# Up block first in seven-product feed-forward cells, three open pairs, and longer DRAM rows for the cells' weights

## The chip, the cores and the metric

One Trainium2 chip, all 8 cores, one launch. Each core computes one prompt stream and two sample streams with the whole set of weights; nothing passes between cores. The metric is the device time in microseconds of the slowest core.

## What is computed

One encoder layer, for 8 prompt streams of 8192 frames (one per core) and 16 sample streams of 32 frames, D = 1024, FFN width 2816. Cut to what matters:

```python
z = x @ w_in                                   # u | v | B | C | x_in
v = layernorm per head(v);  a = u * (masked W_s mixes v over 128 frames + b_s)
b = gb * causal_conv3(gc * xin)
x = layernorm(ALPHA * x + concat(a, b) @ w_out)
p = softmax((x @ w_q) @ mem_k.T / 16);  x = layernorm(ALPHA * x + (p @ mem_v) @ w_mem_o)
f = (silu(x @ w_gate) * (x @ w_up)) @ w_down   # the change is here
x = layernorm(ALPHA * x + f)
```

## The kernel before, in words

A core works through 16 tiles of 512 frames. Part A of a tile (`run_A`) is the input projection with mixers, the output projection, attention scores, and the attention output, its weights in a ring of three 1 MB slots (`ra`). Part B (`run_B`) is the feed-forward block: 11 cells of 256 FFN columns (`gate_up` or `gate_up_7`), then `down` in six pieces. Their weights go through the ring `rb` of 16 units of 128 x 1024 elements, 256 KB each. Part A of tile t+1 runs interleaved with part B of tile t.

In tiles 0 and 1 a cell is plain (32 matmuls of 512 columns). From tile 2 on it is made of seven products instead of eight (a Winograd form of the 2 x 2 block product): `gate_up_7` issues seven groups `prod` of 8 matmuls of 256 columns. The four weight blocks of a cell are a11, a12, a22 (parts `gu` 0 to 2) and a21; four sums of them, s1 to s4 (parts `gs` 0 to 3), are made by VectorE in tile 2 (`weight_sums`, line 981), and four differences of the activations (T1, T3, T4, in `early`, and one in F2) by `row_sums` in each tile. The products accumulate in a pair of PSUM banks, ba and bb, with evacuations between them: ScalarE copies M1 from bb into `s5`, then ba into bb (bank<-bank), applies silu to ba for the gate half into `sg`; VectorE adds bb and s5 into ba and into s5, and two multiplications write hT (the last one's line is 1032). There are two buffers s5 and four sg, two per cell, so two cells' pairs can be open.

Weights are cast to 16 bits once, by GpSimd's DMAs from `w_pieces` (line 633), stored by SP into a DRAM scratch `wsc` of rows of 8 KB per partition and piece (line 609), and loaded from it later: whole pieces into `ra` (line 628), single units with rows of 2 KB into `rb` (`load_unit`, line 616). The sums are stored as pieces gs0 to gs10 in tile 2. A cell of a later tile loads seven single units in the order in which the products use them (`CELL`).

The other transfers: SP stores y of a tile in four parts (line 1062) and loads the next x, 2 MB, into the same buffer (line 688), after the last of these stores has landed. GpSimd loads the transposed x (line 673). From tile 3 on ScalarE issues DMA transposes of the layer-normed rows (line 774, F<-xb), eight a tile.

The order of the instructions on each of the five queues is written out by a planner (`Sched.order`), an event simulation with priorities (`S.prio`, lower first, plus `dprio`) and durations (`c_v`, `c_a`, `c_mm`). It models buffers by name (`buf`): an operation that writes a buffer depends on all its former writers and readers, DMAs among them. What it emits is static: each engine runs its list in order and waits on semaphores. Most instructions are recorded through `Resolving.call`, line 89, so rows of the profile are told apart by their tiles.

Of the kernel before, what the change touches and what calls it, by code (L numbers as in the profile page):

```python
# [8 lines left out]
BF16 = mybir.dt.bfloat16  # L9
FP16 = mybir.dt.float16  # L10
AF = mybir.ActivationFunctionType
ALU = mybir.AluOpType
# [117 lines left out]
class Sched:  # L130
# [73 lines left out]
    def order(self):  # L204
# [81 lines left out]
        while ev:  # L286
# [44 lines left out]
            if o.dma:  # L331
                occ = 1.0 if e == "gpsimd" else 0.08
                rings[e].append([o.nbytes, t + occ + 0.6, o])
                dma_step(t)
            else:
                occ = o.dur
                if e == "scalar" and o.table is not None:
                    if table is not None and o.table != table:
                        occ += 1.4
                    table = o.table  # L340
                o.fin = t + occ
# [89 lines left out]
KV_PIECES = ["m0", "m1", "n0", "n1"]  # L431
SUM_PIECES = ["gs%d" % j for j in range(NF // 2)]
STORE_AT = {"in_v": 2, "in_c0": 2, "in_c1": 2, "in_c2": 2, "in_c3": 2, "out0": 2, "out1": 2}
# [8 lines left out]
def build(NT, debug=False):  # L442
# [33 lines left out]
    widx = {n: i for i, n in enumerate(W_PIECES)}  # L476
    SP_PIECES = A_PIECES + B_PIECES + KV_PIECES + SUM_PIECES
    sidx = {n: i for i, n in enumerate(SP_PIECES)}
    wsc = nc.dram_tensor("wsc", [len(SP_PIECES), 128, 4096], BF16, kind="Internal").ap()

    with contextlib.ExitStack() as st:
        def T(name, shape, dt):
            return st.enter_context(nc.sbuf_tensor(name, shape, dt))
# [54 lines left out]
        TB = [early[:, i * 1024:(i + 1) * 1024].bitcast(FP16).rearrange("p (k n) -> p k n", k=4) for i in range(3)]  # L538
        s5 = [early_t[:, 1536 + i * 512:2048 + i * 512] for i in range(2)]
        guard_t = T("guard", [1, 1], F32)  # L540
        def bank(p):
# [44 lines left out]
        def units(n, step):  # L586

            u = -(-rctr["B"] // step) * step % NU
            while u + n > NU and step > 1 or any(("B", (u + i) % NU) in pinned for i in range(n)):
                u = (u + step) % NU  # L590
            rctr["B"] = u + n
            return [(u + i) % NU for i in range(n)]

        def unit(u):
            return rb[:, u * 1024:(u + 1) * 1024], buf("ringB%d" % u)
# [16 lines left out]

        def load_unit(name, n, u, dprio=-0.35):

            src, (dst, b) = wsc[sidx[name]], unit(u)
            op("sync", lambda e: e.dma_start(out=dst, in_=src[:, n * 1024:(n + 1) * 1024]), [buf("wsc_" + name)], [b],  # L616
               dma="rB%d" % u, nbytes=1 << 18, dprio=dprio)

        def piece(r, name, t, dprio=-0.35):
            i, dst, b = slot(r)  # L620
            nco = piece_cols(name)
            gu = name[:2] == "gu"
            if name in stored and r == "B":
                for n in range(nco // 1024):
                    load_unit(name, n, i + n, dprio)
            elif name in stored:
                src = wsc[sidx[name]]
                op("sync", lambda e: e.dma_start(out=dst[:, 0:nco], in_=src[:, 0:nco]), [buf("wsc_" + name)], [b],
                   dma="r%s%d" % (r, i), nbytes=256 * nco, dprio=dprio)
            else:  # L630
                src = wp[widx[name]]
                to = dst[:].bitcast(FP16) if gu else dst
                op("gpsimd", lambda e: e.dma_start(out=to[:, 0:nco], in_=src[:, 0:nco]), [], [b],
                   dma="f%s%d" % (r, i), nbytes=512 * nco, pkt=16, dprio=dprio)
                if t == 0:
                    buf("ld_" + name).writers = [S.ops[-1]]
                if name in sidx and t >= STORE_AT.get(name, 0):
                    store(name, dst, b, "w%s%d" % (r, i), nco)
            return (dst[:].bitcast(FP16) if gu else dst), b

        CELL = (("gs", 0), ("gu", 0), ("gu", 1), ("gs", 1), ("gs", 2), ("gs", 3), ("gu", 2))

        def cell_units(j):

            out = {}
            for (kind, n), u in zip(CELL, units(7, 1)):
                load_unit("%s%d" % (kind, j), n, u)
                v, b = unit(u)
                out[kind, n] = (v.bitcast(FP16), b)
            return out  # L650

        def cell_parts(rg, brg, sm, bsm):
            return {(kind, n): ((rg, sm)[kind == "gs"][:, n * 1024:(n + 1) * 1024], (brg, bsm)[kind == "gs"][n]) for kind, n in CELL}

# [136 lines left out]
        def in_proj_v(c, rg, brg, parts=None):  # L791
# [19 lines left out]
            for s in range(4):  # L811
                bk, bb = bank(c.pl)
                for k0, k1, bp in parts:
                    MM([(bk[:], c.F0[:, k, s * 128:(s + 1) * 128], rg[:, k * 512:(k + 1) * 512], k == 0, k == 7) for k in range(k0, k1)],
                       [buf(c.pre + "F0_%d" % s), brg, bp], [bb], 512)

                def out(i, h, bk=bk, bb=bb, s=s):
                    A(lambda e: e.activation(out=c.vh[:, s, h * 128:(h + 1) * 128], in_=bk[:, h * 128:(h + 1) * 128],
                                             func=AF.Identity, scale=rs[i][:, h:h + 1], bias=nm[i][:, h:h + 1]),
                      [bb, buf("rs%d" % i), buf("nm%d" % i)], [buf(c.pre + "vh%d" % s)], 128)  # L820
                sgu_v(bk, bb, 128, out)

        def in_proj_c(c, m, rg, brg):
# [39 lines left out]
            else:  # L863
                A(lambda e: e.activation(out=halo_p[:, m, :], in_=cx3[:, 0, L:L + 2], func=AF.Copy), [bcx], [buf("halo_p%d" % m)], 2)
            A(lambda e: e.activation(out=ac3, in_=cx3[:, :, 0:L], func=AF.Copy, scale=smallT[:, w0:w0 + 1]), [bcx, buf("small")], [bac], n)
            for k in (1, 2):
# [75 lines left out]
        def plain(g, f2, k):  # L942

            b_ = ((0, 1), (3, 2))[g][k // 4]
            return slice(b_ * 1024 + (k % 4) * 256 + f2 * 128, b_ * 1024 + (k % 4) * 256 + (f2 + 1) * 128)
# [27 lines left out]
        def weight_sums(j, rg, brg):  # L973
# [6 lines left out]
            for o_, x_, y_, f_ in ((s1, a21, a22, ALU.add), (s3, a11, a21, ALU.subtract), (s2, s1, a11, ALU.subtract), (s4, a12, s2, ALU.subtract)):  # L980
                V(lambda e, o_=o_, x_=x_, y_=y_, f_=f_: e.tensor_tensor(out=o_, in0=x_, in1=y_, op=f_), [brg] + ([b] if f_ is ALU.subtract else []), [b], 512)
            store("gs%d" % j, raw, b, "wB%d" % i)
            return dst, b
# [13 lines left out]
        def gate_up_7(c, j, w):  # L997
# [7 lines left out]
            def prod(bk, w, x, reads, writes, first):  # L1005
# [7 lines left out]
                op("tensor", fn, reads, writes, dur=c_mm(8, 256))  # L1013
            i5, ia, ib = rot("s5", 2), rot("sg", NSG), rot("sg", NSG)
            b5, bsa, bsb = buf("s5_%d" % i5), buf("sg%d" % ia), buf("sg%d" % ib)
            pair = lambda x: x.rearrange("p (f n) -> p f n", f=2)
            bh = [buf("hT%d" % f) for f in (2 * j, 2 * j + 1)]
            prod(bb, s1, t1, [bs1, buf("T1")], [bbb, bba], True)
            A(lambda e: e.activation(out=s5[i5], in_=bb[:], func=AF.Copy), [bbb], [b5], 512)
            prod(ba, a11, b11, [ba11] + F2b[:2], [bba], True)  # L1020
            A(lambda e: e.activation(out=bb[:], in_=ba[:], func=AF.Copy), [bba], [bbb], 512)
            prod(ba, a12, b21, [ba12] + F2b[:2], [bba], False)
            prod(bb, s2, t2, [bs2] + F2b[2:], [bbb], False)
            A(lambda e: e.activation(out=sg[ia][:], in_=ba[:], func=AF.Silu), [bba], [bsa], 512, table="silu")
            V(lambda e: e.tensor_tensor(out=ba[:], in0=bb[:], in1=s5[i5], op=ALU.add), [bbb, b5], [bba], 512)
            prod(bb, s3, t3, [bs3, buf("T3")], [bbb], False)
            prod(ba, s4, b22, [bs4] + F2b[2:], [bba], False)
            V(lambda e: e.tensor_tensor(out=s5[i5], in0=bb[:], in1=s5[i5], op=ALU.add), [bbb, b5], [b5], 512)
            A(lambda e: e.activation(out=sg[ib][:], in_=ba[:], func=AF.Silu), [bba], [bsb], 512, table="silu")
            prod(bb, a22, t4, [ba22, buf("T4")], [bbb], False)  # L1030
            V(lambda e: e.tensor_tensor(out=hT[:, 2 * j:2 * j + 2, H1], in0=pair(bb[:]), in1=pair(sg[ia][:]), op=ALU.mult), [bbb, bsa], bh, 512)
            V(lambda e: e.tensor_tensor(out=hT[:, 2 * j:2 * j + 2, H2], in0=pair(s5[i5]), in1=pair(sg[ib][:]), op=ALU.mult), [b5, bsb], bh, 512)

# [254 lines left out]
        def run_B(tiles, t):  # L1288
            n = NF // 2
            for j in range(n):  # L1290
# [14 lines left out]
                if t == T_SUMS:  # L1305
                    w = cell_parts(rg, brg, *weight_sums(j, rg, brg))
                for c in tiles:
# [54 lines left out]
def make_in_maps(inputs, NT):  # L1362
# [29 lines left out]
    for j in range(NF // 2):  # L1392
        sl = slice(j * 256, (j + 1) * 256)
        blocks = [kpn(w) for w in (wg[0:512, sl], wg[512:1024, sl], wu[512:1024, sl], wu[0:512, sl])]
        pieces[W_PIECES.index("gu%d" % j)] = np.concatenate(blocks, axis=1)
# [55 lines left out]
```

How the kernel before makes its waits and increments, by code:

```python
                def body(eng, ops=ops, e=e):  # L401
                    view = Resolving(eng)
                    waited = {}
                    dwaited = {}
                    for o in ops:
                        for pe_, d in o.best.items():
                            if waited.get(pe_, 0) < d.sig:
                                eng.wait_ge(sems[pe_], d.sig)
                                waited[pe_] = d.sig
                        for s, c in o.dmadeps.items():
                            if dwaited.get(s, 0) < c:
                                eng.wait_ge(dsems[s], c)
                                dwaited[s] = c
                        inst = o.fn(view if o.leases else eng)
                        if o.dma:
                            inst.then_inc(dsems[o.stream], 16)
                        elif o.signal:
                            inst.then_inc(sems[e], 1)
                    if e == final_wait_eng:
                        for s, c in total.items():
                            if dwaited.get(s, 0) < c:
                                eng.wait_ge(dsems[s], c)
```

## Time and profile before

| What | us |
|---|---|
| median of three runs | 3643.74 |
| lowest, highest run | 3566.81, 3689.93 |
| the profiled execution | 3604.81 |
| its span on the slowest core (3) | 3603.3 |
| spans of the eight cores | 3561.5 to 3603.3 |

The profile is of one execution, on its slowest core. Busy time of TensorE is modelled from pipelined matmuls. PEclk is the clock granted to TensorE as a share of 2.4 GHz. In a row of waits, the instruction named first waited for the one behind the arrow.

### The profile page before, as it was taken

What the parts mean: (1) busy time and instruction counts of PE and PEld (TensorE: products, weight loads), DVE (VectorE), ACT (ScalarE), POOL (GpSimd) and SP (SyncE); (2) the same over time, 40 slices, a digit from 0 to 9 for tenths busy, and PEclk for the clock granted to TensorE, in tenths of its full rate; (3) what the DMA queues carried; (4) which work ended last, traced back from release to release, by engine and by line L of the source; (5) the groups of instructions that cost most, each with busy time, mean ns of one, the idle gap of its engine ahead of it and who ended that gap; (6) DMA issues with size and microseconds to landing.
All of it is one profiled execution on the core that took longest, in us unless ns stands there. A gap on an engine that the chain in (4) does not pass through costs nothing.

```text
span 3603.3 us, 59509 instructions; the slowest of 8 cores (3561.5 to 3603.3 us)
## 1 busy us (share of the span) xinstructions
PE 3243.4 (90%) x19332; PEld 1878.9 (52%) x19332; DVE 1970.8 (55%) x3564; ACT 1071.3 (30%) x1781; POOL 381.3 (11%) x357
## 2 busy tenths in 40 slices
PE   7989999869989897998989899897988899899887
PEld 3544444544555645555555555555555464555564
DVE  5753435645646565554746655464564656456443
ACT  4452123142232422313232232322323242232320
POOL 2111101001001010100101110010110101010000
PEclk9999988978899999999989999998999999999987
DMA  9879887786777869687786877868787786968684
GB/s 180 165 170 198 188 221 195 214 160 182 224 207 205 221 184 256 183 233 199 187 232 196 234 211 224 206 184 223 196 225 216 208 222 187 247 185 224 178 230 122
DMA packets 367182, 731.43 MB, mean 203 GB/s; under 512 B 138464, under 2 KB 138592, under 8 KB 335520
## 3 DMA queue, kind: packets, MB, share of 16 engines
q1 hardware_dynamic: 243664, 623.12, 59.7%
q0 software_dynamic: 12240, 75.13, 12.3%
q10 hardware_dynamic: 110976, 29.37, 6.3%
q8 instruction: 163, 2.67, 0.3%
q14 instruction: 139, 1.14, 0.1%
HBM read 694.73 MB, written 76.43 MB: 214 GB/s over the span
## 4 chain that ended last, share of the span: by engine, by line
PE 68%; DMA 24%; issue 2%; DVE 1%; ACTq 1%; ACT 1%; SPq 1%; POOL 1%; DVEq 0%; POOLq 0%
PE bank L89 68%; DMA rb<-wsc 6%; DMA y_prompt<-xbuf 5%; DMA F<-xb 5%; DMA xbuf<-x_prompt 5%; DMA rb<-w_pieces 2%; ACTq L774 1%; DMA F<-x_prompt_t 0%; ACT xb L770 0%; POOL rs L718 0%; SPq L616 0%; DMA WTS<-w_s_t_s 0%; DVE bank L89 0%; DVE xin L867 0%; SPq L1062 0%
## 5 line engine op out<-in xcount | busy, mean ns | idle before, releaser
L89 PE MATMUL bank<-F,rb 128*128 128x256 f16 (+2 forms) x5696 | 828.3, 301 | 108.5 <-ACT bank L89 92.7
L89 PEld LDWEIGHTS bank<-F,rb 128*128 128x128 f16 (+1 forms) x5696 | 580.7, 103 | 303.8 <-issue 150.9
L89 PE MATMUL bank<-F,ra 128*128 128x512 bf16 x2944 | 698.9, 389 | 34.1 <-DMA F<-xb 32.3
L89 PE MATMUL bank<-rb,hT 128*128 128x512 bf16 (+1 forms) x2832 | 659.4, 392 | 29.2 <-DMA rb<-wsc 29.2
L89 PE MATMUL bank<-early,rb 128*128 128x256 f16 (+2 forms) x4112 | 509.2, 276 | 140.9 <-DMA rb<-wsc 76.4
L718 POOL TENSOR_TENSOR rs<-ve,mhalf 128x1 f32<-128x1 f32 (+1 forms) x260 | 333.1, 1283 | 2274.0 <-DVE ve L716 2159.8
L89 PE MATMUL bank<-ra,F 128*128 128x512 bf16 x2400 | 566.8, 390 | 5.4 <-DMA F<-x_prompt_t 2.5
L89 DVE SCALAR_TENSOR_TENSOR xbuf<-xbuf,bank 128x512 f32<-128x512 f32 x384 | 256.1, 672 | 488.3 <-PE bank L89 298.2
L89 PEld LDWEIGHTS bank<-early,rb 128*128 128x128 f16 (+1 forms) x4112 | 386.9, 102 | 246.6 <-issue 159.6
L89 PEld LDWEIGHTS bank<-F,ra 128*128 128x128 bf16 x2944 | 289.9, 100 | 377.2 <-issue 95.6
L89 PEld LDWEIGHTS bank<-rb,hT 128*128 128x128 bf16 (+1 forms) x2832 | 282.5, 100 | 385.5 <-issue 123.7
L89 ACT ACTIVATE sg<-bank 128x512 f32<-128x512 f32 (+1 forms) x363 | 211.6, 587 | 663.8 <-PE bank L89 633.9
L89 PEld LDWEIGHTS bank<-ra,F 128*128 128x128 bf16 x2400 | 239.5, 100 | 278.7 <-issue 49.8
L741 DVE BATCH_NORM_STATS2 stat<-xbuf 128x6 f32<-128x512 f32 x384 | 262.8, 689 | 16.0
L770 ACT ACTIVATE xb<-xbuf 128x1024 bf16<-128x1024 f32 (+1 forms) x128 | 135.0, 1056 | 454.5 <-DVE mv L744 350.4
L749 DVE SCALAR_TENSOR_TENSOR xbuf<-xbuf,rs,lnb 128x1024 f32<-128x1024 f32 x192 | 244.5, 1276 | 2.7 <-POOL rs L718 2.7
L89 DVE TENSOR_TENSOR hT<-bank,sg 128x512 bf16<-128x512 f32 x198 | 135.6, 686 | 201.1 <-PE bank L89 200.2
L747 DVE SCALAR_TENSOR_TENSOR xbuf<-xbuf,mv,lng 128x1024 f32<-128x1024 f32 x192 | 244.7, 1275 | 0.2 <-issue 0.2
L89 ACT ACTIVATE early<-bank 128x512 f32<-128x512 f32 (+3 forms) x164 | 96.2, 596 | 415.0 <-PE bank L89 341.0
L89 DVE TENSOR_TENSOR bank<-bank,early 128x512 f32<-128x512 f32 x154 | 105.5, 692 | 163.6 <-PE bank L89 130.7
L939 DVE TENSOR_TENSOR F<-F,rden 128x512 bf16<-128x512 bf16 x128 | 82.9, 688 | 195.2 <-ACT rden L937 185.0
L89 ACT ACT_TABLE_LOAD x102 | 130.9, 1283 | 107.5 <-PE bank L89 106.8
(116 smaller groups left out, 1700.1 us busy)
## 6 DMA issues: line engine op xcount, KB each, us to landing
rb<-wsc SPq DMA_DIRECT2D x1377, 256.0 KB, 8.4
ra<-wsc SPq DMA_DIRECT2D x147, 1024.0 KB, 6.9
rb<-w_pieces POOLq DMA_DIRECT2D x34, 1024.0 KB, 14.8
y_prompt<-xbuf SPq DMA_DIRECT2D x64, 512.0 KB, 12.1
xbuf<-x_prompt SPq DMA_DIRECT2D x14, 2048.0 KB, 13.3
wsc<-rb SPq DMA_DIRECT2D x27, 1024.0 KB, 12.2
F<-x_prompt_t POOLq DMA_DIRECT2D x14, 1024.0 KB, 13.3
ra<-w_pieces POOLq DMA_DIRECT2D x13, 1024.0 KB, 14.5
```

The source lines that it names most:

```text
L89: return f(*[r(x) for x in a], **{n: r(x) for n, x in k.items()})
L718: P(lambda e: e.tensor_tensor(out=rs[i][0:SP, 0:n], in0=ve[i][0:SP, 0:n], in1=mhalf[0:SP, 0:n], op=ALU.pow), [buf("ve%d" % i), buf("mhalf" ...
L741: V(lambda e: e.bn_stats(out=stat[i][0:SP, half, :], in_=xv[:, sl]), [bx[half]], [buf("stat%d" % i)], 512)
L747: V(lambda e: e.scalar_tensor_tensor(out=xv, in0=xv, scalar=mv[i][0:SP, 0, 0:1], in1=lng[li][0:SP, :], op0=ALU.subtract, op1=ALU.mult), bx ...
L749: V(lambda e: e.scalar_tensor_tensor(out=xv, in0=xv, scalar=rs[i][0:SP, 0:1], in1=lnb[li][0:SP, :], op0=ALU.mult, op1=ALU.add), bx + [buf( ...
L770: A(lambda e: e.activation(out=row, in_=xv, func=AF.Copy), bx, [buf("xb%d" % j)], 1024)
L774: op("scalar", lambda e: e.dma_start_transpose(out=dst, in_=row), [buf("xb%d" % j)], [b_dst], dma="tr%d" % j, nbytes=1 << 19, pkt=4)
L939: V(lambda e, mc=mc: e.tensor_tensor(out=FT[:, 2 * h + mc, :], in0=FT[:, 2 * h + mc, :], in1=rden[:, 0:n], op=ALU.mult), [buf("rden"), buf ...
```

## The change

It has four parts. The blocks of a `gu` piece are ordered up, up, gate, gate (they were gate, gate, up, up), and `plain` is changed to match; in `gate_up_7` the block in ba, which is finished early, is then the up half: it is copied to SBUF instead of passed through silu, and silu is applied in place to the gate results, once in SBUF (p5) and once in PSUM (bb), after which two multiplications write hT. A cell takes one of three pairs of buffers (`side`: four sg and two s5). The weights of a cell lie in a DRAM tensor `wcell` in the order of use, rows of 14 KB, and are loaded by three DMAs, with rows of 4, 4 and 6 KB into adjacent units of `rb`; tile 2 writes `wcell` with five DMAs per cell, gu blocks included. Pieces of `w_down` (and gu pieces) in `wsc` are loaded two units at a time; `units` no longer wraps round inside a group. And the planner books more time for three ScalarE operations: a DMA issue, the vh evacuation and the first convolution product.

```diff
-                occ = 1.0 if e == "gpsimd" else 0.08
+                occ = {"gpsimd": 1.0, "scalar": 1.25}.get(e, 0.08)
...
+    wcell = nc.dram_tensor("wcell", [NF // 2, 128, 7168], BF16, kind="Internal").ap()
...
+        side = [(sg[0][:], "sg0", sg[1][:], "sg1"), (sg[2][:], "sg2", sg[3][:], "sg3"), (s5[0], "s5_0", s5[1], "s5_1")]
...
-            u = -(-rctr["B"] // step) * step % NU
-            while u + n > NU and step > 1 or any(("B", (u + i) % NU) in pinned for i in range(n)):
-                u = (u + step) % NU
+            u = -(-rctr["B"] // step) * step
+            while True:
+                if u + n > NU:
+                    u = 0
+                if not any(("B", u + i) in pinned for i in range(n)):
+                    break
+                u += step
...
-                for n in range(nco // 1024):
-                    load_unit(name, n, i + n, dprio)
+                for n in range(0, nco // 1024, 2):
+                    load_units(name, n, i + n, min(2, nco // 1024 - n), dprio)
...
-        CELL = (("gs", 0), ("gu", 0), ("gu", 1), ("gs", 1), ("gs", 2), ("gs", 3), ("gu", 2))
+        CELL = ((("gs", 0), ("gu", 0)), (("gu", 1), ("gs", 1)), (("gs", 2), ("gs", 3), ("gu", 2)))
...
-            for (kind, n), u in zip(CELL, units(7, 1)):
-                load_unit("%s%d" % (kind, j), n, u)
+            for group in CELL:
+                n = len(group)
+                us = units(n, 1)
+                dst, src = rb[:, us[0] * 1024:(us[0] + n) * 1024], wcell[j][:, at * 1024:(at + n) * 1024]
+                op("sync", lambda e, dst=dst, src=src: e.dma_start(out=dst, in_=src), [buf("cell%d" % j)], [buf("ringB%d" % u) for u in us],
+                   dma="rB%d" % us[0], nbytes=n << 18, dprio=-0.35)
...
+            for kind, n, w, at in (("gu", 0, 2, 1), ("gu", 2, 1, 6), ("gs", 0, 1, 0), ("gs", 1, 1, 3), ("gs", 2, 2, 4)):
+                src, b = (rg, brg) if kind == "gu" else (sm, bsm)
+                op("sync", lambda e, src=src, n=n, w=w, at=at: e.dma_start(out=wcell[j][:, at * 1024:(at + w) * 1024], in_=src[:, n * 1024:(n + w) * 1024].bitcast(BF16)),
+                   [b[n + i] for i in range(w)], [buf("cell%d" % j)], dma="w" + b[n].name, nbytes=w << 18, dprio=0.05)
...
-                      [bb, buf("rs%d" % i), buf("nm%d" % i)], [buf(c.pre + "vh%d" % s)], 128)
+                      [bb, buf("rs%d" % i), buf("nm%d" % i)], [buf(c.pre + "vh%d" % s)], 310)
...
-            A(lambda e: e.activation(out=ac3, in_=cx3[:, :, 0:L], func=AF.Copy, scale=smallT[:, w0:w0 + 1]), [bcx, buf("small")], [bac], n)
+            A(lambda e: e.activation(out=ac3, in_=cx3[:, :, 0:L], func=AF.Copy, scale=smallT[:, w0:w0 + 1]), [bcx, buf("small")], [bac], n + 100)
...
-            store("gs%d" % j, raw, b, "wB%d" % i)
...
-            A(lambda e: e.activation(out=s5[i5], in_=bb[:], func=AF.Copy), [bbb], [b5], 512)
+            A(lambda e: e.activation(out=p5, in_=bb[:], func=AF.Copy), [bbb], [b5], 512)
...
-            A(lambda e: e.activation(out=sg[ia][:], in_=ba[:], func=AF.Silu), [bba], [bsa], 512, table="silu")
-            V(lambda e: e.tensor_tensor(out=ba[:], in0=bb[:], in1=s5[i5], op=ALU.add), [bbb, b5], [bba], 512)
+            A(lambda e: e.activation(out=up, in_=ba[:], func=AF.Copy), [bba], [bup], 512)
+            V(lambda e: e.tensor_tensor(out=ba[:], in0=bb[:], in1=p5, op=ALU.add), [bbb, b5], [bba], 512)
             prod(bb, s3, t3, [bs3, buf("T3")], [bbb], False)
             prod(ba, s4, b22, [bs4] + F2b[2:], [bba], False)
-            V(lambda e: e.tensor_tensor(out=s5[i5], in0=bb[:], in1=s5[i5], op=ALU.add), [bbb, b5], [b5], 512)
-            A(lambda e: e.activation(out=sg[ib][:], in_=ba[:], func=AF.Silu), [bba], [bsb], 512, table="silu")
+            V(lambda e: e.tensor_tensor(out=p5, in0=bb[:], in1=p5, op=ALU.add), [bbb, b5], [b5], 512)
+            A(lambda e: e.activation(out=p5, in_=p5, func=AF.Silu), [b5], [b5], 512, table="silu")
             prod(bb, a22, t4, [ba22, buf("T4")], [bbb], False)
-            V(lambda e: e.tensor_tensor(out=hT[:, 2 * j:2 * j + 2, H1], in0=pair(bb[:]), in1=pair(sg[ia][:]), op=ALU.mult), [bbb, bsa], bh, 512)
-            V(lambda e: e.tensor_tensor(out=hT[:, 2 * j:2 * j + 2, H2], in0=pair(s5[i5]), in1=pair(sg[ib][:]), op=ALU.mult), [b5, bsb], bh, 512)
+            A(lambda e: e.activation(out=bb[:], in_=bb[:], func=AF.Silu), [bbb], [bbb], 512, table="silu")
+            V(lambda e: e.tensor_tensor(out=hT[:, 2 * j:2 * j + 2, H2], in0=pair(ba[:]), in1=pair(p5), op=ALU.mult), [bba, b5], bh, 512)
+            V(lambda e: e.tensor_tensor(out=hT[:, 2 * j:2 * j + 2, H1], in0=pair(bb[:]), in1=pair(up), op=ALU.mult), [bbb, bup], bh, 512)
...
-        blocks = [kpn(w) for w in (wg[0:512, sl], wg[512:1024, sl], wu[512:1024, sl], wu[0:512, sl])]
+        blocks = [kpn(w) for w in (wu[0:512, sl], wu[512:1024, sl], wg[512:1024, sl], wg[0:512, sl])]
```

## Rows read from the trace of the kernel before

**Rows 1.** The cores view, both dies (span, mean granted clock)

```profile
die 0 (median of its cores): 3592.8 us, clock 0.937
die 1 (median of its cores): 3570.3 us, clock 0.945
```

**Rows 2.** The page, part 1: busy time, share of the span, instructions

```profile
PE 3243.4 (90%) x19332; PEld 1878.9 (52%) x19332; DVE 1970.8 (55%) x3564; ACT 1071.3 (30%) x1781; POOL 381.3 (11%) x357
```

**Rows 3.** Waits of TensorE in 1021:3342: releaser, us in total, times, longest

```profile
PE bank L89 <- DMA rb<-wsc: 99.2, 27, 8.6
PE bank L89 <- ACT bank L89: 76.9, 21, 10.4
PE bank L89 <- DVE bank L89: 26.7, 14, 4.2
PE bank L89 <- DMA F<-xb: 21.4, 9, 4.2
```

**Rows 4.** Timeline of TensorE in one period: start, us, instruction [idle before, releaser]

```profile
2219.45 1.04 PE L89 MATMUL bank<-early,rb 128*128 128x256 f16 x8
2225.23 1.87 PE L89 MATMUL bank<-early,rb 128*128 128x256 f16 x8 [4.74 <-DMA rb<-wsc]
...
2236.46 1.03 PE L89 MATMUL bank<-early,rb 128*128 128x256 f16 x8 [2.56 <-DVE bank L89]
...
2288.16 3.57 PE L89 MATMUL bank<-F,rb 128*128 128x256 f16 x16 [10.43 <-ACT bank L89]
```

**Rows 5.** Timeline of the SP queue, same period

```profile
2206.92 0.78 SPq L1062 DMA_DIRECT2D y_prompt<-xbuf  x1
...
2221.93 0.38 SPq L688 DMA_DIRECT2D xbuf<-x_prompt  x1
```

**Rows 6.** Waits of the SP queue in 1021:3342

```profile
SPq L412 <- DMA y_prompt<-xbuf: 77.1, 22, 6.7
```

**Rows 7.** Timeline of VectorE, same period

```profile
2234.90 0.69 DVE L89 SCALAR_TENSOR_TENSOR xbuf<-xbuf,bank 128x512 f32<-128x512 f32 x1 [14.49 <-DMA xbuf<-x_prompt]
```

**Rows 8.** Timeline of ScalarE's DMA issues, same period

```profile
2263.67 1.23 ACTq L774 DMA_TRANSPOSE F<-xb  x1
...
2268.70 8.78 ACTq L774 DMA_TRANSPOSE F<-xb  x1
...
2279.26 7.23 ACTq L774 DMA_TRANSPOSE F<-xb  x1
```

**Rows 9.** Windows: busy us by engine, then granted clock, DMA share, GB/s

```profile
2226.20:2229.00 2.80, 2.80 (x16) 1.84 (x14) 0.00 (x0) 0.75 (x2) 0.00 (x0) 0.60 0.97 331
```

**Rows 10.** Groups of instructions by form, whole span

```profile
L89 ACT ACTIVATE bank<-bank 128x512 f32<-128x512 f32 x154 | 89.7, 582 | 97.8 <-PE bank L89 94.1 <-ACT early L89 0.4
```

**Rows 11.** DMA queues in 2020:2028, then in 1409:1412: packets, MB, share

```profile
q1 hardware_dynamic: 872, 2.64, 94.0%
...
q1 hardware_dynamic: 204, 1.17, 102.9%
```

**Rows 12.** Windows: the stretch of tile 2's feed-forward cells

```profile
665.00:807.00 142.00, 105.55 (x674) 69.11 (x672) 77.36 (x121) 51.62 (x73) 6.93 (x6) 0.86 0.88 193
```

**Rows 13.** Instructions on wsc in 600:811: DMA to landing

```profile
DMA to landing us min/median/max: 3.1/8.9/19.5
```

**Rows 14.** DMA issues in 600:810: count, KB, median us to landing

```profile
y_prompt<-xbuf SPq DMA_DIRECT2D x4, 512.0 KB, 4.2
```

**Rows 15.** DMA queues in 2072:2080, SP's q1 and ScalarE's q10

```profile
q1 hardware_dynamic: 1297, 2.36, 84.5%
q10 hardware_dynamic: 1589, 0.40, 23.8%
```

**Rows 16.** DMA queues in 2156:2160

```profile
q1 hardware_dynamic: 140, 1.03, 89.7%
q10 hardware_dynamic: 364, 0.09, 10.2%
```

More of the change, by code:

```diff
@@ L431 @@
 KV_PIECES = ["m0", "m1", "n0", "n1"]
-SUM_PIECES = ["gs%d" % j for j in range(NF // 2)]
 STORE_AT = {"in_v": 2, "in_c0": 2, "in_c1": 2, "in_c2": 2, "in_c3": 2, "out0": 2, "out1": 2}
@@ L476, in build @@
     widx = {n: i for i, n in enumerate(W_PIECES)}
-    SP_PIECES = A_PIECES + B_PIECES + KV_PIECES + SUM_PIECES
+    SP_PIECES = A_PIECES + B_PIECES + KV_PIECES
     sidx = {n: i for i, n in enumerate(SP_PIECES)}
     wsc = nc.dram_tensor("wsc", [len(SP_PIECES), 128, 4096], BF16, kind="Internal").ap()
+    wcell = nc.dram_tensor("wcell", [NF // 2, 128, 7168], BF16, kind="Internal").ap()
     with contextlib.ExitStack() as st:
@@ L586, in units @@
         def units(n, step):
-            u = -(-rctr["B"] // step) * step % NU
-            while u + n > NU and step > 1 or any(("B", (u + i) % NU) in pinned for i in range(n)):
-                u = (u + step) % NU
+            u = -(-rctr["B"] // step) * step
[5 more added lines that the diff above has]
+                u += step
             rctr["B"] = u + n
-            return [(u + i) % NU for i in range(n)]
+            return list(range(u, u + n))
         def unit(u):
@@ L611, in store, with load_units @@
             stored.add(name)
[L613 to L617, printed above, removed]
+        def load_units(name, n, u, w, dprio):
+            src = wsc[sidx[name]]
+            op("sync", lambda e: e.dma_start(out=rb[:, u * 1024:(u + w) * 1024], in_=src[:, n * 1024:(n + w) * 1024]), [buf("wsc_" + name)],
+               [buf("ringB%d" % (u + i)) for i in range(w)], dma="rB%d" % u, nbytes=w << 18, dprio=dprio)
         def piece(r, name, t, dprio=-0.35):
@@ L639, in piece, with cell_parts @@
             return (dst[:].bitcast(FP16) if gu else dst), b
-        CELL = (("gs", 0), ("gu", 0), ("gu", 1), ("gs", 1), ("gs", 2), ("gs", 3), ("gu", 2))
+        CELL = ((("gs", 0), ("gu", 0)), (("gu", 1), ("gs", 1)), (("gs", 2), ("gs", 3), ("gu", 2)))
         def cell_units(j):
-            out = {}
-            for (kind, n), u in zip(CELL, units(7, 1)):
-                load_unit("%s%d" % (kind, j), n, u)
-                v, b = unit(u)
-                out[kind, n] = (v.bitcast(FP16), b)
-            return out
-        def cell_parts(rg, brg, sm, bsm):
-            return {(kind, n): ((rg, sm)[kind == "gs"][:, n * 1024:(n + 1) * 1024], (brg, bsm)[kind == "gs"][n]) for kind, n in CELL}
+            out, at = {}, 0
+            for group in CELL:
[4 more added lines that the diff above has]
+                   dma="rB%d" % us[0], nbytes=n << 18, dprio=-0.35)
+                for name, u in zip(group, us):
+                    v, b = unit(u)
+                    out[name] = (v.bitcast(FP16), b)
+                at += n
+            return out
+        def cell_parts(j, rg, brg, sm, bsm):
+            out, at = {}, 0
+            for group in CELL:
+                for kind, n in group:
+                    src, b = (rg, brg) if kind == "gu" else (sm, bsm)
+                    out[kind, n] = (src[:, n * 1024:(n + 1) * 1024], b[n])
+            for kind, n, w, at in (("gu", 0, 2, 1), ("gu", 2, 1, 6), ("gs", 0, 1, 0), ("gs", 1, 1, 3), ("gs", 2, 2, 4)):
+                src, b = (rg, brg) if kind == "gu" else (sm, bsm)
+                op("sync", lambda e, src=src, n=n, w=w, at=at: e.dma_start(out=wcell[j][:, at * 1024:(at + w) * 1024], in_=src[:, n * 1024:(n + w) * 1024].bitcast(BF16)),
+                   [b[n + i] for i in range(w)], [buf("cell%d" % j)], dma="w" + b[n].name, nbytes=w << 18, dprio=0.05)
+            return out
         S.prio = -2.0
@@ L942, in plain @@
         def plain(g, f2, k):
-            b_ = ((0, 1), (3, 2))[g][k // 4]
+            b_ = ((3, 2), (0, 1))[g][k // 4]
             return slice(b_ * 1024 + (k % 4) * 256 + f2 * 128, b_ * 1024 + (k % 4) * 256 + (f2 + 1) * 128)
@@ L1013, in prod @@
                 op("tensor", fn, reads, writes, dur=c_mm(8, 256))
-            i5, ia, ib = rot("s5", 2), rot("sg", NSG), rot("sg", NSG)
-            b5, bsa, bsb = buf("s5_%d" % i5), buf("sg%d" % ia), buf("sg%d" % ib)
+            i5 = rot("side", 3)
+            (p5, b5), (up, bup) = (side[i5][0], buf(side[i5][1])), (side[i5][2], buf(side[i5][3]))
             pair = lambda x: x.rearrange("p (f n) -> p f n", f=2)
@@ L1305, in run_B @@
                 if t == T_SUMS:
-                    w = cell_parts(rg, brg, *weight_sums(j, rg, brg))
+                    w = cell_parts(j, rg, brg, *weight_sums(j, rg, brg))
                 for c in tiles:
```

## The prediction

> **What bounds the kernel now.** I read the cores first [rows 1]: the two dies lie 0.6% apart, so the profiled core 3 speaks for all. Then the page [rows 2]. TensorE is busy for 3243 of 3603 us, VectorE 55% and ScalarE 30%, so the kernel is TensorE with about 360 us of gaps. The page's slices look even, and the timeline repeats itself every 211 us or so from tile 3 on. The window 1021:3342 holds eleven such periods, and the waits of TensorE in it [rows 3] sum to 224 us, 20.4 us a tile: DMA rb<-wsc 9.0, ACT bank 7.0, DVE bank 2.4, DMA F<-xb 1.9. All four touch something the change edits.
>
> One period in detail [rows 4] shows where they fall. At 2225 the first product of a feed-forward cell waits 4.7 us for its weights. The SP queue says why [rows 5]: SP issued the last store of y, then five weight loads, sat until 2221.93 for that store to land (in SP's own list of waits [rows 6] the ones on y_prompt are 77.1 us over 22 times), issued the 2 MB load of x, and only then the next weights. At 2236 TensorE waits 2.6 us for the addition on VectorE. VectorE itself stood still for 14.5 us on the load of x [rows 7], and the addition is behind that instruction. At 2288 it waits 10.4 us for a ScalarE copy. ScalarE was held by two issues of DMA transposes, 8.78 and 7.23 us [rows 8], where a free issue takes 1.23 (the first two of this tile did). So three of the four waits are DMA in origin: the queue of weights, y and x is full, and the transposes share the 16 engines with it.
>
> Each gap costs more than itself. The eight matmuls before the gap at 2225 take 1.04 us and the eight after it 1.87 us [rows 4]; the granted clock of 2226.2:2229 is 0.60 of full speed [rows 9], so most of that stretch ran at 1.2 GHz after TensorE had been idle. A gap that goes takes some 0.8 us of this with it.
>
> **The change part by part.** Sums are against the profiled execution's own 3604.8 us (span 3603.3 plus 1.5 around it). That is 1.1% under the 3643.7 us median of the three runs, whose ends are 3566.8 and 3689.9.
>
> (1) Up block first. The blocks of a piece are reordered on the host: nothing on the chip. In the seven products ScalarE did per cell two copies and two silus from PSUM. It now does three copies and two silus: one instruction more, 0.6 us [rows 10]. 11 cells in 14 tiles make 154 x 0.6 = 92 us of ScalarE, at 30% busy. VectorE keeps two additions and two multiplications. The critical copy (bank<-bank, which TensorE needs next) has the same place in the order. What is longer is the tail: the last product was followed by one multiplication (0.69, as a 512-column operation of VectorE takes in [rows 7]), and now by a silu (0.58, as the copy from bank to bank) and a multiplication, with a hop between, so one bank is held some 0.8 us longer and the other, once freed by the silu after s4, waits for addition, silu and multiplication, 1.3 us more. With 8 banks and cells of seven products of 1.04 us [rows 4] this is beside other products. Its bounds are 0 and 0.8 us in each of 154 cells (123 us, if no other pair were open); I take 0.5 us a tile, since a third pair is open.
>
> (2) Three pairs instead of two. Scratch for a third cell gives TensorE work that needs no evacuation: up to four products, some 4 us, before the addition is wanted. It can cover part of the short waits for ACT and DVE, not the end of a 10 us block, and only where the planner wrote such an order; the planner doesn't know that a transpose issue may block. It now books 1.25 us for it, which is its price when free, and more than before for the vh and xin instructions. Bounds: 0 to the whole 9.4 us a tile of ACT and DVE waits. I take 2.5 us, nearer the low end, because the large gap is the blocked issue.
>
> (3) Longer rows. A cell is loaded by 3 DMAs with rows of 4, 4 and 6 KB instead of 7 of 2 KB, and the pieces of w_down in pairs. SP issues 45 loads into rb a tile instead of 99. Issue time is no gain, since SP mostly waits for TensorE. The bytes are the same. The rate in a full stretch [rows 11]: 2020:2028, 872 packets of 3.0 KB in the mean, moves 2.64 MB in 8 us, 330 GB/s at 94% busy; 1409:1412, 204 packets of 5.7 KB, moves 1.17 MB in 3 us, 390 GB/s at a full share. Per busy share that is 351 against 379, 8%, and 18% as they stand. For rows of 4 to 6 KB instead of 2 I take 10%. The y store and the load behind it land after some 15 us (2206.92 to 2221.93) and 13 us (2221.93 to the end of VectorE's wait at 2234.90), 28 us a tile, so x and the weights after it are some 2.8 us sooner: I book 3 us of the 9.0 us for rb (the smaller waits for rb gain too) and 1.5 us of the 2.4 us of DVE bank. Bounds: 0 and 11.4 us a tile.
>
> (4) Coarser ring. A group can be loaded when its last unit is free, and its first product can start when all of it has landed: 512 KB instead of 256 KB before the first product, 0.26 MB / 330 GB/s = 0.8 us, on a lead that the way from issue to landing (8.9 us in the median of tile 2's stage, [rows 13]) has nearly eaten. It hits the product after the load of x, and the start of w_down. Cost 0.8 to 2 us a tile, I take 1.
>
> (5) The clock after the gaps: two gaps of five fewer or shorter, 1 us a tile.
>
> Steady part: -3 -1.5 -2.5 -1 +1 +0.5 = -6.5 us in each of the 13 tiles that load cells, -85 us.
>
> (6) Tile 2. It now writes seven units a cell instead of four: 33 more units, 8.7 MB, at the 193 GB/s of that stage [rows 12], 45 us of queue. More important, the five stores of a cell write one planner buffer, and each depends on the one before, so SP must wait for a landing four times a cell, 44 times. Behind such a wait stand the loads of the next cell, w_in pieces and the next x. A DMA of this queue lands after 3.1 us at best and 8.9 in the median [rows 13]. The cells of tile 2 take 142 us (665:807). 44 x 3.1 = 136 us would just fit, costing nothing; 44 x 8.9 = 392 would add 250 us. Half-sized stores at little load are nearer the low end: y's 512 KB landed after 4.2 us in this stage [rows 14]. 44 x 4.2 = 185, 43 us over the stage; the cells' two chains overlap in part, so I take +45 with the bytes included.
>
> Sum: 3604.8 - 85 + 45 = 3565 us, 1.1% faster.
>
> **The rivals.**
>
> A. The queue was the whole matter. Then faster rows undo nearly all waits for rb and DVE and the block of the transposes too, since they stand in the same queue: 20.4 us a tile less a rest of 8, 12 us with 1.5 of clock, x 13 = 176, less 45 in tile 2: 3475 us, 3.6% faster. For it: the stretch of tile cells 2226 to 2290 runs with the DMA engines 97% busy at its start [rows 9]. Against it: the wait for y's landing before x stays in the order.
>
> B. The transposes are starved: the slower case. In 2072:2080 the queue of ScalarE passes 1589 packets and that of SP 1297 [rows 15], so nearly one small packet for one of 2 KB. 84.5% and 23.8% of 8 x 16 engine-us over these counts are 83 and 19 ns, 102 ns a pair. If turns stay one for one and SP's packets become 4.7 KB in the mean (83 x 4.7 / 2 = 195 ns), a pair takes 214 ns, and four transposes take twice as long. Then the blocked issues and the landing double: 7.0 + 1.9 = 8.9 us more a tile, x 13 = 116 us, + 45 in tile 2, less 4.5 x 13 = 58 for what is left of (2) to (5): 3708 us, 2.9% slower. It decides once a transpose issue of ScalarE commonly exceeds 14 us. Against it: beside 8 KB rows (2156:2160) the small packets were 364 against 140, not one for one [rows 16], though their rate, 91 a us, is half of the 199 before.
> The Trainium skill (DMA: Bandwidth & Descriptors, "Queues, rings and completion order") has each DMA engine take turns between queues a whole packet at a time; that rule is what would make B true, for longer packets then take longer turns. The first window agrees, the second only in part.
>
> C. Stores serialised in tile 2 are worse than booked and the rest is covered: 44 waits at 6 us are 264, 122 over the stage, with 85 back: 3604.8 + 37 = 3642 us, 1.0% slower.
>
> D. It does not do what it says: the planner writes the same order with two pairs mostly open, and the rate is bounded elsewhere: 3604.8 - 13 x 1.5 + 45 = 3630 us, 0.7% slower.
>
> **How the numbers follow.** A measurement of this kernel tells about 2% from no change. Forecast 0.48 (of it 0.15 beyond 2% faster, below 3533), A 0.18, B 0.14, C 0.09 (0.03 beyond 2% slower), D 0.11. Faster 0.15 + 0.18 = 0.33; slower 0.14 + 0.03 = 0.17; same, the rest, 0.50. The range, 3455 to 3700, reaches A on one side and nearly B on the other. The likeliest case alone spans 3510 to 3620.
>
> **What would show it.** Right: 45 loads into rb a tile with a larger share under 8 KB; DMA rb<-wsc below 6.5 us a tile; DVE bank near 1; ScalarE 92 us busier; in tile 2 a new wait of SP on DMA wcell<-rb, some 40 times, and a longer stage. Wrong by A: F<-xb issues back at 1.23 us and TensorE's waits below 10 us a tile. Wrong by B: transpose issues over 14 us, ACT bank above 12 us a tile. Wrong altogether: TensorE's busy time itself moves by over 1% at the same clock, or waits on banks that are not in the list now.

## The result, and the profile after

The changed kernel takes 0.955 of the time of the one before (95% interval 0.944 to 0.966): median 3426.7 us against 3614.4 us, 4 runs each, and 0.951 (0.946 to 0.955) in a second session. The ratio leaves out executions in which one die was slowed by a lower granted clock, so it is not the quotient of the two medians. That is 4.5% faster. Applied to the 3604.8 us on which the prediction's sums stand, it gives 3443 us: outside the range of 3510 to 3620 us that the likeliest case had, under the 3455 us at the low end of the whole range, and beyond rival A's 3.6% too. Of the profiled executions, 3603.3 us of span became 3415.4 us, with core 1 the slowest.

The cores view and the page of the changed kernel, its two dies and part 1:

```profile
die 0 (median of its cores): 3372.6 us, clock 0.970
die 1 (median of its cores): 3369.6 us, clock 0.972
```

```profile
PE 3130.8 (92%) x19332; PEld 1839.1 (54%) x19332; DVE 1980.5 (58%) x3564; ACT 1112.0 (33%) x1903; POOL 389.1 (11%) x357
```

TensorE issues the same 19332 matmuls, and is busy for 112 us less [rows 2]. So more than half of the 188 us is not idle time that went, but matmuls that ran at a higher granted clock: 0.970 against 0.937 and 0.945 of the dies before [rows 1]. The trace of before has a part in this that is not the kernel's: its core 3 stood at 0.81 for some stretches, as this answer of the windows view shows (busy us by engine, then granted clock, DMA share, GB/s). The first line is of the kernel before, the second of the changed one:

```profile
510.00:660.00 150.00, 150.00 (x630) 65.11 (x629) 71.78 (x141) 49.20 (x72) 17.47 (x19) 0.81 0.67 174
...
510.00:660.00 150.00, 146.52 (x773) 71.95 (x772) 94.91 (x177) 57.70 (x88) 21.73 (x21) 1.00 0.85 223
```

The 188 us can be laid out by the times at which SP issues the loads of x. The third one stands at 945.9 us before and at 892.6 us after, so 53 us are gained before the steady part. The eleven periods behind it take 2342.7 and 2240.2 us, 213.0 and 203.7 us each, which is 102 us. The rest, 32 us, is gained behind the last load.

The waits of TensorE in 1000:3200 of the changed kernel, 10.8 of its periods:

```profile
PE bank L89 <- DMA F<-xb: 72.4, 8, 12.7
PE bank L89 <- ACT bank L89: 56.2, 20, 10.1
PE bank L89 <- DVE bank L89: 24.2, 19, 5.9
PE bank L89 <- DMA rb<-wsc: 3.8, 1, 3.8
PE bank L89 <- DMA rb<-wcell: 0.4, 1, 0.4
```

Against [rows 3], per tile: the wait for weights fell from 9.0 to 0.4 us, DVE bank hardly moved (2.4 to 2.2), ACT bank went from 7.0 to 5.2, and the wait for the transposes rose from 1.9 to 6.7. The sum went from 20.4 to 14.5 us.

The SP queue around one load of x, in the timeline of the changed kernel, answers to [rows 5]:

```profile
2108.32 0.85 SPq L1082 DMA_DIRECT2D y_prompt<-xbuf  x1
...
2117.29 0.38 SPq L708 DMA_DIRECT2D xbuf<-x_prompt  x1
```

The last y landed after 9 us instead of 15. VectorE's wait for x, of which [rows 7] shows one case, went from 189.0 us in 13 cases to 43.6 us in 6, over the whole span. This is its row in the waits of VectorE of the changed kernel:

```profile
DVE xbuf L89 <- DMA xbuf<-x_prompt: 43.6, 6, 15.3
```

The issues on ScalarE are not better than in [rows 8] (timeline of ScalarE, DMA issues and what came behind them):

```profile
2354.24 2.32 ACTq L794 DMA_TRANSPOSE F<-xb  x1
2358.37 9.67 ACTq L794 DMA_TRANSPOSE F<-xb  x1
2368.14 0.63 ACT L1048 ACTIVATE sg<-sg 128x512 f32<-128x512 f32 x1 [9.84 <-issue]
```

L1048 is the silu in place. Over the whole span ScalarE stood 141 us behind its own issues (before: 75 us), 107 of them in front of this silu. Tile 2's cells took 138 us (647:785) instead of 142 [rows 12].

### The profile page after: what moved, and what is told of

Read it like the earlier page. It is cut to its first block, busy times and chain, and to the rows that moved or that the text cites. A ratio compares the mean times of both kernels' runs of the same rounds, so it can differ in the third digit from the quotient of the medians.

```text
span 3415.4 us, 57320 instructions; the slowest of 8 cores (3314.7 to 3415.4 us)
## 1 busy us (share of the span) xinstructions
PE 3130.8 (92%) x19332; PEld 1839.1 (54%) x19332; DVE 1980.5 (58%) x3564; ACT 1112.0 (33%) x1903; POOL 389.1 (11%) x357
## 4 chain that ended last, share of the span: by engine, by line
PE 75%; DMA 16%; issue 2%; ACTq 2%; DVE 2%; ACT 1%; POOL 1%; SPq 0%; DVEq 0%; POOLq 0%
PE bank L89 75%; DMA F<-xb 6%; DMA y_prompt<-xbuf 2%; ACTq L794 2%; DMA xbuf<-x_prompt 2%; DMA rb<-w_pieces 2%; DMA rb<-wcell 1%; DMA rb<-wsc 1%; DMA wcell<-rb 1%; POOL rs L738 1%; DMA ra<-w_pieces 1%; ACT xb L790 0%; DVE xbuf L769 0%; ACT sg L89 0%; DVE rb L1001 0%
## 5 line engine op out<-in xcount | busy, mean ns | idle before, releaser
L89 PE MATMUL bank<-F,rb 128*128 128x256 f16 (+2 forms) x5696 | 781.2, 291 | 74.3 <-ACT bank L89 59.8
L89 PEld LDWEIGHTS bank<-F,rb 128*128 128x128 f16 (+1 forms) x5696 | 563.2, 100 | 250.2 <-issue 92.2
L89 PE MATMUL bank<-rb,hT 128*128 128x512 bf16 (+1 forms) x2832 | 632.9, 380 | 9.7 <-DVE mv L748 6.0
L89 PE MATMUL bank<-early,rb 128*128 128x256 f16 (+2 forms) x4112 | 479.4, 268 | 82.9 <-DVE bank L89 28.8
L89 PE MATMUL bank<-ra,F 128*128 128x512 bf16 x2400 | 545.5, 381 | 3.1 <-ACT F L89 1.4
L89 DVE TENSOR_TENSOR hT<-bank,sg 128x512 bf16<-128x512 f32 x250 | 169.9, 688 | 188.3 <-ACT sg L1048 83.2
L89 ACT ACTIVATE sg<-bank 128x512 f32<-128x512 f32 (+1 forms) x261 | 151.2, 582 | 384.2 <-PE bank L89 376.9
L89 ACT ACTIVATE bank<-bank 128x512 f32<-128x512 f32 x308 | 178.3, 581 | 142.8 <-PE bank L89 131.5
L89 ACT ACTIVATE xin<-bank 128x512 f32<-128x512 f32 (+1 forms) x68 | 39.1, 575 | 330.6 <-PE bank L89 325.9
L89 ACT ACTIVATE F<-bank 128x512 bf16<-128x512 f32 (+3 forms) x160 | 105.6, 671 | 103.3 <-PE bank L89 102.5
```

The source lines that it names most:

```text
L89: return f(*[r(x) for x in a], **{n: r(x) for n, x in k.items()})
```

## The experiments

All ratios are to the kernel before, on the same chip and in the same session, with 95% intervals. Kernels with the same first letter ran in one session; between letters the chip can differ.

| Kernel | What it is | Ratio |
|---|---|---|
| e1_dma | before + DMA part | 0.9475 (0.941, 0.954) |
| e2_pairs | before + compute part | 0.9885 (0.983, 0.994) |
| e3_plan | before + planner durations | 0.999 (0.994, 1.004) |
| e4_noplan | changed, planner part undone | 0.953 (0.949, 0.958) |
| f1_rows2k | e1, cells' rows 2 KB, unit by unit | 0.926 (0.918, 0.934) |
| f2_singles | e1, seven DMAs a cell | 0.936 (0.930, 0.943) |
| f3_down1 | e1, w_down in single units of 2 KB rows | 0.960 (0.953, 0.968) |
| f4_free | e1, stores independent | 0.948 (0.941, 0.954) |
| g1_layout | before, rb pieces unit by unit | 0.934 (0.929, 0.939) |
| g2_pitch10 | before, wsc rows 10 KB apart | 0.936 (0.931, 0.942) |
| g3_blocks | e1, 4/4/6 KB rows, each group in one run | 0.960 (0.954, 0.967) |
| g4_allunits | f1, w_down unit by unit too | 0.924 (0.918, 0.931) |
| h1_pitch16 | changed, wcell rows 16 KB apart | 0.953 (0.944, 0.962) |
| i2_after2k | changed, cells' rows 2 KB, unit by unit | 0.933 (0.927, 0.939) |
| h3_all | i2, w_down unit by unit too | 0.920 (0.915, 0.925) |
| i1_pitch16 | before, wsc rows 16 KB apart | 0.963 (0.954, 0.971) |
| h4_after | the changed kernel once more | 0.951 (0.946, 0.955) |
| h2_after2k | the same kernel as i2 | none |

**The parts one by one.** e1, e2 and e3 take the hunks of the diff for one part each into the kernel before; e4 takes the planner's three numbers out of the changed one.

> The kernel before with the DMA part alone (wcell, groups of 2, 2 and 3 units, pairs of units for w_down, five stores per cell in tile 2). Theory 1, the queue carries the gain: its rows alone give 3 to 4% (0.960 to 0.970 of before), and TensorE's wait for weights falls from 112 us to under 30. Theory 2, the open pairs and the planner's order carry it: under 1.5%, with the wait for weights lower but the time lost again to ACT and DVE banks.

> The kernel before with the compute part alone (up block first, silu in place, three pairs), loads of single units with 2 KB rows as before. Theory 1: within 1% of before, waits for rb of 100 us or more remain. Theory 2: 2.5% faster or more, DVE bank and ACT bank waits down by a third.

> The kernel before with the planner's three durations alone (ScalarE's DMA issue 1.25 us, vh and first convolution product longer). Theory 1: within 1%. Theory 2: up to 2% faster, since the order then leaves room for the transposes' issues; ACT bank waits fall from 93 us to some 60.

> The changed kernel with the planner's three durations put back. If the durations only correct an order that has slack, 0.955 to 0.965 of before. If they are needed for the pairs to pay, 0.97 or more, with ACT bank waits back at 90 us.

The DMA part alone has the whole gain (0.9475; its interval overlaps those of the whole change), the compute part 1.2% by itself and nothing on top that these runs can tell, the planner's numbers nothing in either place. In e3 the ACT bank waits did not fall (113 us over the span, before 93), so the 1.25 us for an issue did not help the order.

**Rows, groups, stores.** The first of these keeps every engine's order and the number of DMAs of e1, and changes where the units lie:

```diff
-    wcell = nc.dram_tensor("wcell", [NF // 2, 128, 7168], ...)
+    wcell = nc.dram_tensor("wcell", [NF // 2, 7, 128, 1024], ...)
-    dst, src = rb[:, us[0] * 1024:(us[0] + n) * 1024], wcell[j][:, at * 1024:(at + n) * 1024]
+    dst, src = rb[...].rearrange("p (u c) -> p u c", u=n), wcell[j, at:at + n].rearrange("u p c -> p u c")
```

> The DMA part alone, the same order of instructions on every engine, the same number of DMAs and the same groups, but wcell laid out unit by unit, so that each DMA of a cell moves rows of 2 KB. Theory 1a, the length of the rows is what counts: most of the gain of 5.3% goes, ratio to before 0.98 or more, with y's stores back at 12 us to landing. Theory 1b, the grouping and the order counts (fewer issues, other release points): ratio within 1% of 0.9475.

I had expected the gain to go with the rows. It grew by 2.3% instead, so neither 1a nor 1b holds. f2 gives each unit a group of its own (`CELL` of seven groups of one), f3 puts `for n in range(nco // 1024)` with width 1 back for w_down, f4 gives each store a buffer `cell%d_%d` and lets the loads depend on all five.

> The DMA part alone, but every unit of a cell loaded by a DMA of its own from wcell (seven of 2 KB rows, as before; rows for w_down still 4 KB). Theory 1a: 0.98 or more of before, as with 2 KB rows in groups. Theory 1b: 0.98 or more as well if the number of DMAs counts. It tells the coarser ring: if grouping costs the 1 us a tile that I booked, this one is 0.4% faster than the grouped one with rows of 2 KB.

f2 is no faster than f1 (0.936 against 0.926, the intervals overlap). Its rows also lie 14 KB apart where f1's units lie in one run, so this is not a test of the grouping alone. The pair g4 and g1 below has all units in one run, and the one with groups is not slower either (0.924 against 0.934; it has the order of the DMA part besides). No cost of grouping shows.

> The DMA part alone, but the pieces of w_down loaded by single units with rows of 2 KB, while the cells keep 4 and 6 KB. w_down is 22 of 99 units of a tile. By theory 1a a fifth of the gain goes, ratio 0.955 to 0.96. If the stretch before the loads of x decides, in which w_down's loads end, more: 0.965.

> The DMA part alone, but the five stores of a cell write five planner buffers, so that none waits for another. If the serial stores cost the 45 us that I booked for tile 2, 1% faster: 0.937. If they are covered, within 0.3% of 0.9475.

f3 is 1.4% behind e1, and 1.4% behind f4, which ran beside it, with intervals that just touch. So 2 KB rows 8 KB apart seem bad for w_down too: its loads of 256 KB landed after 9.1 us, where e1's of 512 KB took 7.4. (f3 also issues twice as many loads there.) f4 equals e1: the serial stores cost nothing.

**The place in DRAM.** What f1 and e1 share, and the kernel before lacks, is that a cell's units are not read from rows 8 KB apart. Two kernels test that in the kernel before, without any other part of the change. g2 is one number:

```diff
-    wsc = nc.dram_tensor("wsc", [len(SP_PIECES), 128, 4096], BF16, kind="Internal").ap()
+    wsc = nc.dram_tensor("wsc", [len(SP_PIECES), 128, 5120], BF16, kind="Internal").ap()
```

g1 stores the rb pieces in `wsu`, `[pieces, 4, 128, 1024]`, and `load_unit` reads `src[n]`.

> The kernel before, every engine's order unchanged, single-unit loads with rows of 2 KB as before; only the place in DRAM changes: the pieces of the rb ring lie unit by unit, so a load reads 256 KB in one run (before: 128 rows of 2 KB, 8 KB apart). Theory 3, the place in DRAM carries the gain: 0.94 to 0.955 of before, the mean time of a 2 KB packet from 123 to about 105 ns. Theory 1, row length: nothing, 0.99 to 1.0.

> The kernel before with one number changed: wsc rows are 10 KB apart instead of 8 (2 KB of padding), so single-unit loads read 2 KB of every 10. Theory 3a, a distance of 8 KB makes the rows of the 16 DMA engines meet in the same part of the memory: 0.945 to 0.96, as g1. Theory 3b, it is the gaps between the rows as such (a run of 256 KB is read better than pieces): 0.99 to 1.0.

Of theory 3a the first half holds, that the distance of 8 KB is what costs: 2 KB of padding that nothing reads make the kernel 6.4% faster, more than the whole change. That rows meet in the same part of the memory is its guess at a reason, and no run shows it. Both kernels gained a little more than I had expected. The queue rows of g2 (page, part 3 and 6: packets, MB, share; KB each, us to landing):

```profile
q1 hardware_dynamic: 243664, 623.12, 58.7%
...
rb<-wsc SPq DMA_DIRECT2D x1377, 256.0 KB, 6.0
y_prompt<-xbuf SPq DMA_DIRECT2D x64, 512.0 KB, 7.1
```

and of the kernel before:

```profile
q1 hardware_dynamic: 243664, 623.12, 59.7%
...
rb<-wsc SPq DMA_DIRECT2D x1377, 256.0 KB, 8.4
y_prompt<-xbuf SPq DMA_DIRECT2D x64, 512.0 KB, 12.1
```

The same packets and bytes; the engines' time for a packet is share x 16 x span / packets, 141 ns before and 129 ns with g2. These 9%, in a queue that is at times nearly full (94% in the first stretch of [rows 11]), bring y's landing from 12.1 to 7.1 us, and that was the chain behind the waits for weights and x. TensorE's waits in g2, 1000:3000:

```profile
PE bank L89 <- ACT bank L89: 37.5, 20, 4.7
PE bank L89 <- DMA F<-xb: 28.2, 9, 5.2
PE bank L89 <- DVE bank L89: 15.6, 11, 2.6
PE bank L89 <- DMA rb<-wsc: 9.8, 9, 2.6
```

These are 91 us in 2000, where the kernel before had 224 in 2321. ACT bank fell as well, from 7.0 us a tile to some 3.7, with ScalarE's program untouched. The transposes run on the same 16 DMA engines: ScalarE stood 43 us behind its issues instead of 75, and a transpose landed after 6.3 us instead of 7.3 in the median.

Which distances are bad? i1 pads the kernel before to 16 KB (8192 for 4096), h1 the changed one (`wcell` of 8192 columns for 7168).

> The kernel before with wsc rows 16 KB apart instead of 8: 2 KB rows at twice the distance, nothing else changed. If a distance that is a multiple of 8 KB is what costs (as the padding to 10 KB suggests), 0.99 or more of before, perhaps over 1. If only the dense case costs, in which four units of a piece share 8 KB, 0.935 to 0.945 as with 10 KB.

> The changed kernel with one number changed: the rows of wcell are 16 KB apart instead of 14 (2 KB of padding), same rows of 4 and 6 KB, same order everywhere. If it is the distance of 8 KB or a multiple that costs, and not only for rows of 2 KB: 0.975 to 0.99 of before, the gain of the change gone. If 4 and 6 KB rows are safe at any distance: 0.955, as the changed kernel.

For rows of 2 KB, 16 KB lies between what I had given as the two cases: 3.7% faster than 8 KB, 2.8% slower than 10 KB. Rows of 4 and 6 KB run alike at 14 and 16 KB (0.953 against 0.951 of the changed kernel in the same session).

**The length of the rows.** g3 keeps e1's rows of 4, 4 and 6 KB but lays each group out as one run (`wcell` flat, a block of 128 x n x 1024 per group; gu 0 and gu 1 are stored by two DMAs). Against f1 it has the rows' length as the difference, but for that store.

> The DMA part with rows of 4, 4 and 6 KB, each group's block lying in one run instead of in rows 14 KB apart. Against the same with rows of 2 KB (0.926) it has the length of the rows alone as the difference. If long rows starve the transposes (wait for F<-xb 58 to 100 us against 12), 0.945 to 0.955; if the run of 14 KB rows was what cost, 0.925 to 0.93.

It measured 0.960, 3.7% behind f1 and slower than either case expected. Waits of TensorE in 1000:3000, first of g3_blocks:

```profile
PE bank L89 <- DMA F<-xb: 72.5, 7, 13.0
PE bank L89 <- ACT bank L89: 34.1, 17, 7.7
```

then of f1_rows2k:

```profile
PE bank L89 <- ACT bank L89: 12.9, 17, 1.6
PE bank L89 <- DMA F<-xb: 12.4, 3, 4.8
```

TensorE waits 60 us more for the transposes in the same stretch when the packets beside them are long. They land after 7.1 us instead of 6.4 in the median, and after 30.8 instead of 22.8 at the most. The direction is rival B's: the longer the packets of one queue, the later the other. By the rule of the Trainium skill cited there (DMA: Bandwidth & Descriptors, "Queues, rings and completion order"), that a DMA engine takes turns between queues a whole packet at a time, the trace agrees in direction. But the page's packet is a bundle of mostly 9 to 17 descriptors, where the profile counts single rows, so that the rule asks for no turns of one for one.

The traces do not show such turns either. I took all stretches of 4 us in 1100:2900 with over 100 of the transposes' packets and SP's queue over 60% busy. For each packet of SP there were 1.7 small ones in f1 and 3.0 in g3 (1.3 in the kernel before, 2.7 in the changed one). The small ones passed at 152 a us in f1 and at 127 in g3, a sixth fewer and not half as many. How the turns are taken stays open. Nor does a long wait for the transposes follow from long rows in every order: e4_noplan, with the changed kernel's rows, has 5.7 us of it in 1000:3000, but 62.6 us on ScalarE's banks and 49.3 us on weights, for the same ratio as the changed kernel.

**The whole change with this repaired, and the last comparison.** i2 (h2_after2k is the same kernel; it has no interval, and its fastest two executions took 3318 and 3338 us) is the changed kernel with f1's layout, h3 with g4's. g4 and h3 use `wsu` for w_down and the gu pieces also.

> The DMA part with rows of 2 KB and everything of the rb ring unit by unit, w_down too (still two units a DMA). By theory 3 the rest of the gain comes in: 0.915 to 0.925. If w_down's rows of 4 KB at 8 KB were no worse than this, 0.926 as without it.

> The changed kernel with rows of 2 KB for the cells, wcell laid out unit by unit; same order, same number of DMAs. Theory: without the long rows the transposes get their turns, 0.93 of before (2.5% under the changed kernel), the wait for F<-xb from 72 us to under 30. If the compute part pays once the weights come in time, below 0.926.

> The changed kernel with rows of 2 KB for the cells, unit by unit, once more with more rounds, since the ratio of h2_after2k had no interval. 0.925 to 0.93 of before; 0.926 is what the DMA part alone had with this layout, so below 0.92 would say that the compute part pays by itself, above 0.935 that it costs.

> As the last, with w_down and the gu pieces laid out unit by unit too: the whole change with the best place and rows found. 0.915 to 0.925 of before. If the compute part costs rather than pays, above 0.924, which the DMA part alone with this layout had.

> The changed kernel once more, on the chip of the other three, as what they are compared with: 0.955 of before.

Repaired, the change goes from 0.951 to 0.933 and 0.920. Against their partners without the compute part (f1 0.926, g4 0.924) the intervals overlap both times: the compute part with its three pairs is worth nothing that these runs can tell. h3_all is the fastest of all kernels run, 8.0% under the kernel before and 3.2% under the changed one in the same session; g4_allunits is not told from it.

## Why the prediction was wrong

The direction was right, the size was not: 1.1% was forecast and 4.5% came.

(3), the rows, failed, in its reason and its size. I read "longer rows are faster" from two stretches whose rows differ in length, 2 KB units against whole 8 KB rows [rows 11]. But the 2 KB rows there lie 8 KB apart, the 8 KB rows lie side by side. The comparison moved two things at once, and I put the difference down to the wrong one. g2 has 2 KB rows and loses nothing; g3 has long rows in one run and is slower than f1. The 3 us a tile booked for the weights were 8.6; DVE bank, where I booked 1.5, moved by 0.2. The true term is: units away from rows 8 KB apart, +6.4% (g2), of which the long rows took some 2 to 4% back (e1 against f1: 2.3%, the changed kernel against i2: 1.8%; g3 against f1: 3.7%).

Rival B had the direction of what takes this back, at a smaller price: F<-xb rose by 4.8 us a tile, and ACT bank, which was to double, fell to 5.2. Its turns of one for one, its figure of 8.9 us more and its sign for the whole were wrong. Nearest in size was A, by luck: the effect in the queue was one that I had not found, and what was to show A, transpose issues back at 1.23 us, is absent. (A's sum comes to 3474 us, not 3475.) C and D, both slower, are out by the sign.

(5), the clock, was booked at 1 us a tile. Over ten periods between loads of x (1158.3:3288.6 before, 1101.9:3132.8 after) TensorE's busy time a tile fell from 191.5 to 188.1 us, 3.4 us, at a granted clock of 0.96 and 0.97. A period got 10 us shorter, where 6.5 were booked for a tile. So most of the 112 us of busy time does not come from the steady tiles: 57 us of it lie before the third load of x (865.2 us busy at 0.91 before, 808.5 at 0.97 after) and 17 behind the last. The trace of before had its lowest clocks in these two, 0.91 and 0.87. A trace of the same program but for the planner's numbers, e3_plan, had 0.955 on both dies, the third load of x at 903 us and a span of 3556 us; by it some 47 us of the 188 are the profiled execution's own. The ratio of the runs does not rest on that trace.

(1) and (2), the compute part: 0.5 us cost and 2.5 us gain a tile were booked, 26 us net. With the old layout it measured 1.2% (e2), about 41 us; with the weights in time, nothing. ScalarE got 41 us busier in the profile rather than 92: silu and copies sum to 94 us more, as priced, but in the new order 74 table loads of 1.28 us stand where 106 did, which gives 41 us back. Some 12 us are not accounted for.

(4), the coarser ring: 1 us a tile was booked; neither f2 against f1 nor g1 against g4 shows a cost. (6), tile 2: +45 us was booked. SP did wait for the landings, as foretold, 27 times and 57 us in all (waits of the SP queue, whole span, changed kernel):

```profile
SPq L412 <- DMA wcell<-rb: 57.0, 27, 8.2
```

but the stage of the cells took no longer, and f4 without these waits runs as e1. That the next loads wait for units to come free anyway would explain it; no run tests that. So two terms pulled the forecast towards no change: 45 us of cost that was none, and a gain on the weights booked at less than half.

Open stays why rows of 2 KB at 8 KB are slow and at 16 KB half so; no run looked at addresses. That g3, in one run, is behind e1 (0.960 against 0.948, intervals that only touch, in different sessions) is not explained either; its order differs by one store.

## What to carry to other kernels

When two kinds of transfer in a trace differ in speed, list all in which they differ (row length, distance between rows, neighbours in the queue) before one is priced; a padding of the DRAM tensor is a one-number test and comes first. A scratch tensor that is stored whole and read in parts should lie in the order of the parts. And longer rows are no gain in themselves beside another queue with small packets on which the critical path waits. Compare profiles over the same number of periods, found from an instruction that comes once in each: a stretch of round numbers holds another count of tiles in another kernel.

## What the runs showed of the hardware

- Reading 2 KB from each of 128 rows 8 KB apart cost 141 ns of engine time a packet over the queue, with 10 KB between rows 129 ns; with 16 KB the kernel was 3.7% faster, with 10 KB 6.4%. Rows of 4 and 6 KB showed no difference between 14 and 16 KB.
- In a DMA queue near its limit, this 9% moved the landing of a 512 KB store behind it from 12.1 to 7.1 us.
- Rows of 4 and 6 KB instead of 2 KB, each group in one run, made the kernel 3.7% slower beside a queue of DMA transposes (g3 against f1).
- Issues of DMA transposes held ScalarE for up to 9.7 us before and 13.3 us in the changed kernel, where a free one takes 1.23. Other work of ScalarE stood behind them for 75 us before and 141 us after. The rows alone do not make that difference: e2_pairs, with the old rows and the new compute part, has 138 us, e1_dma, with the new rows and the old compute part, 99 us, and f1_rows2k 52 us.
